# Local attention on one core: scores and values two units at a time, and another order of the softmax steps

## The chip, the cores and the metric

The kernel runs on one core of one Trainium2 chip. The metric is the device time of one execution in microseconds (us), the median of several. Three runs of the kernel before gave 1345.87, 1345.98 and 1346.46 us.

## The reference, cut to what matters

Two layers over 512 tokens of width 1024, float32. Layer 0 mixes tokens with a Mamba-2 scan, layer 1 with the local attention below. Both layers also attend to 256 memory tokens (4 heads of 128), project the joined outputs back and add a squared-ReLU MLP. The change is in layer 1, with one line in layer 0.

```python
# q (b, 8 chunks, 64 queries, 4 kv heads, 4 q heads each, 64); kb, vb: own and previous chunk (128 keys)
scores = jnp.einsum("bcqkgd,bcjkd->bkgcqj", qb, kb) * (64 ** -0.5) + bias   # keys before 0: -inf
m = jnp.maximum(jnp.max(scores, axis=-1, keepdims=True), sink)
p = jnp.exp(scores - m)
denom = jnp.sum(p, axis=-1, keepdims=True) + jnp.exp(sink - m)
out = jnp.einsum("bkgcqj,bcjkd->bcqkgd", p / denom, vb)
# mixed = concat(out, memory attention) @ w_out, w_out 1536 x 1024
```

## The kernel before, in words

Each engine has one hand-ordered stream of instructions, and the streams meet at semaphores.

**Projections.** A float32 matrix product is made of three float32r products: high times high, high times low, low times high. Weights come in panels of 128x1024 elements: a DMA fills `raw` (two buffers), ScalarE rounds it into `whi` (line 557), VectorE subtracts to get `wlo` (line 1098), both three panels ahead of use (`ahead`). TensorE works a panel as four **slots**, one for each PSUM bank G[0] to G[3], six matmuls of 512 columns each (line 1696). After each slot `after_bank` may insert other work; its slot number counts from the first slot of block `B_QB`. Slots 0 to 15 project the second half of the queries, 16 to 31 the memory queries, 32 to 55 the output projection `swa_w_out`, which from slot 32 reads attention outputs as its still operand. A bank can be started anew only when its last result is copied out (`bank_free`): for the queries by lines 1571 (VectorE) and 1023 (ScalarE), for the memory queries by line 1030 (ScalarE).

**Local attention, placed between the slots.** A **unit** u (0 to 15) is one chunk of 64 queries for eight of the 16 heads: `hf, c = divmod(u, 8)`. The first chunk has 64 keys, others 128. Its steps are:

- scores, TensorE (line 2143): four matmuls into the first halves of X[0] and X[1]; float32, two records each, on 64 rows of the array;
- scaling and bias, VectorE (line 1603), from X into `sc[u % 2]`; it waits for the transposes of unit u - 2, which read the same buffer;
- maximum and its negatives, VectorE (lines 1611 to 1614);
- exponentials with sums, ScalarE (lines 998 and 1000);
- division, VectorE (lines 1620 to 1622);
- transposes, TensorE (line 2170), into X[2], and the copy into `pT[u % 2]`, ScalarE (line 1014);
- values, TensorE (line 2159), into the first half of X[3]; float32, on 64 columns of the array;
- the outputs' high part, ScalarE (line 1007), and low part, VectorE (line 1590), which are read by the output projection.

**Order.** `W_TURN` puts turn u behind slot 6 + 2u. In turn u TensorE does the scores of u + 2, the values of u - 1 and the transposes of u. VectorE does scaling and maximum of u + 1 (with the low part of u - 2 between them), then the division of u, then the weight piece `wlo` if the turn is the panel's first. ScalarE does the exponentials of u + 1, the weight piece `whi`, the high part of u - 1 and the copy into `pT` of u. The query copies at slots 14 and 16 (`Q_OUT`) and the memory query copies at slots 30 and 32 (`QM_OUT`) come last in their turns on ScalarE; on VectorE those at 14 and 16 stand behind the division. A panel's first turn is the one at slot 4k, with odd u. The memory attention starts behind slot 38.

**Layer 0.** Behind the slots of its output projection the gated outputs are transposed, a tile f at a time, through the one bank X[3] (`y0_tile`, line 1969). ScalarE takes the high part (line 791), VectorE the low part (`y0_lo`, line 1314), and the next tile waits for that. Steps of the memory attention (`memory_step`) go on between them.

Of the kernel before, what the change touches and what calls it, by code (L numbers as in the profile page):

```python
# [31 lines left out]
P = 128  # L32
# [50 lines left out]
Y0_SLOT = {(44 + f, 0): f for f in range(9)} | {(53, 1): 9, (53, 3): 10, (54, 1): 11}  # L83
MA_STEP = {(53, 1): 0, (54, 0): 1, (54, 3): 2, (55, 2): 3, (56, 1): 4, (57, 0): 5, (57, 2): 6, (58, 0): 7}
# [34 lines left out]
W_FIRST = {1: 0, 2: 1}  # L119
# [19 lines left out]
def build(nc, a, out):  # L139
    ctx = ExitStack()  # L140
    with ctx:
# [213 lines left out]
        def _(sp):  # L355
# [110 lines left out]
            for n in range(12):  # L466
                load(v[n % 6, n // 6], B_W1 + n // 4, n % 4)
                if n == 7:
                    sp.wait_ge(a_o, 2 * NCH)
                    gains("norm_mix_post", "norm_mlp_pre", 1, 1)  # L470
# [72 lines left out]
        def _(act):  # L543
# [460 lines left out]
            def w_out(u):  # L1004
                hf, c = divmod(u, NCH)
                act.wait_ge(a_o, u + 1)
                act.activation(y1hi[:, 4 * hf:4 * hf + 4, CH * c:CH * c + CH],
                               X[3][:, 0:256].rearrange("p (r q) -> p r q", r=4), ACT.Copy).then_inc(a_hi, 1)
# [24 lines left out]
            def attention_panel(blk, q):  # L1033
# [6 lines left out]
                for slot in range(first, first + 4):  # L1040
                    if W_FIRST.get(slot) == 0:
                        w_exp(0)
                    u = W_TURN.get(slot)
                    if u is not None:
                        if u + 1 < 2 * NCH:
                            w_exp(u + 1)
# [3 lines left out]
                        if u >= 1:  # L1050
                            w_out(u - 1)
                        w_turned(u)
                    if slot == W_LAST:
                        w_out(2 * NCH - 1)
# [29 lines left out]
        def _(dve):  # L1084
# [283 lines left out]
            def mixer_out_panel(q):  # L1368
# [8 lines left out]
                for b in range(4):  # L1377
# [4 lines left out]
                    f = Y0_SLOT.get((4 * B_W0 + q, b))  # L1382
# [203 lines left out]
            def w_lo(u):  # L1586
                hf, c = divmod(u, NCH)
                where = (slice(None), slice(4 * hf, 4 * hf + 4), slice(CH * c, CH * c + CH))
                dve.wait_ge(a_hi, u + 1)
                dve.tensor_tensor(y1lo[where], X[3][:, 0:256].rearrange("p (r q) -> p r q", r=4),  # L1590
                                  y1hi[where].bitcast(F32), ALU.subtract).then_inc(a_lo, 1)

            def w_scores(u):
# [3 lines left out]
                cols, heads = slice(4 * u, 4 * u + 4), slice(4 * hf, 4 * hf + 4)  # L1597
                dve.wait_ge(a_s, u + 1)
                if u >= 2:
                    dve.wait_ge(a_tr, u - 1)  # L1600
                for g in range(2):
                    s = X[g][:, 0:256].rearrange("p (r n) -> p r n", r=2)
# [5 lines left out]
                if u >= 3:  # L1608
                    w_lo(u - 3)
# [15 lines left out]
            def attention_panel(blk, q):  # L1625
# [6 lines left out]
                for slot in range(first, first + 4):  # L1632
                    if W_FIRST.get(slot) == 0:
                        w_scores(0)
# [620 lines left out]
```

## Time and profile before

| | |
|---|---|
| median of three runs | 1345.98 us (1345.87 to 1346.46) |
| the profiled execution's own time | 1347.32 us |
| its span, first to last instruction | 1345.6 us |
| TensorE busy (PE) | 1330.5 us, 99% of the span |
| VectorE busy (DVE) | 688.0 us, 51% |
| ScalarE busy (ACT) | 586.6 us, 44% |
| GpSimd busy (POOL) | 124.4 us, 9% |
| mean granted TensorE clock | 0.999 |
| chain that ended last | PE 85%, DVE 8%, ACT 4% of the span |

A group's name is line, engine, operation and tile. A busy TensorE counts every matmul from its start to its modelled end, and neighbours overlap. The distance between two starts is what a matmul costs, not its length: a float32r matmul of 512 columns has a record of 0.39 us. An idle time in brackets is what the engine spent with nothing running, and behind the arrow stands what ended it.

### The profile page before, as it was taken

How to read it: one execution, taken by the hardware profiler on the slowest of the kernel's cores; microseconds unless marked ns; L12 is line 12 of the kernel's file. 1: busy time of each engine (PE TensorE's matmuls, PEld its weight loads, DVE VectorE, ACT ScalarE, POOL GpSimd, SP SyncE). 2: the span in 40 equal slices, each digit the busy share in tenths (PEclk: the TensorE clock that was granted, in tenths of full speed). 3: DMA queues.
4: the chain of work that ended last, by engine and by line, in shares of the span. 5: the costliest groups of instructions: out<-in, count | busy, mean ns of one | idle time of the engine just before them, and what ended most of it. 6: DMA issues, size and time to landing. Idle time of an engine off the chain costs nothing.

```text
span 1345.6 us, 18412 instructions
## 1 busy us (share of the span) xinstructions
PE 1330.5 (99%) x6943; PEld 1095.9 (81%) x6943; DVE 688.0 (51%) x1085; ACT 586.6 (44%) x1107; POOL 124.4 (9%) x131
## 2 busy tenths in 40 slices
PE   9999999999999999999999999999999999999998
PEld 7777778887788888888888897777898888888886
DVE  5586677886437543223443364765374432244333
ACT  6645455686435443213432244665364332234321
POOL 0045352761000000000000000000000000000000
PEclk9999999999999999999999999999999999999999
DMA  6343433343432323242232233112223323332231
GB/s 211 97 132 102 124 98 99 108 161 110 157 110 79 98 90 108 94 126 94 94 110 88 69 117 99 51 60 79 78 65 108 109 95 117 102 94 94 94 99 74
DMA packets 75551, 137.75 MB, mean 102 GB/s; under 512 B 6342, under 2 KB 16854, under 8 KB 75478
## 3 DMA queue, kind: packets, MB, share of 16 engines
q1 hardware_dynamic: 71184, 134.76, 31.0%
q10 hardware_dynamic: 4294, 2.00, 0.8%
q8 instruction: 48, 0.79, 0.2%
q14 instruction: 25, 0.20, 0.0%
HBM read 133.41 MB, written 2.93 MB: 101 GB/s over the span
## 4 chain that ended last, share of the span: by engine, by line
PE 85%; DVE 8%; ACT 4%; issue 2%; POOL 1%; DMA 1%; DVEq 0%; ACTq 0%; POOLq 0%
PE G L1696 54%; PE X L1696 12%; PE X L1719 7%; PE G L1769 3%; PE X L1769 3%; DVE conv L1237 2%; PE X L1883 1%; PE X L1874 1%; ACT whi L557 1%; PE X L1957 1%; DVE wlo L1098 1%; ACT sc L1000 1%; DVE sc L1603 1%; PE X L1896 1%; DVE satt L1611 1%
## 5 line engine op out<-in xcount | busy, mean ns | idle before, releaser
L1098 DVE TENSOR_TENSOR wlo<-raw,whi 128x1024 fp32r<-128x1024 f32 x223 | 274.7, 1237 | 458.6 <-ACT whi L557 457.7
L557 ACT ACTIVATE whi<-raw 128x1024 fp32r<-128x1024 f32 x223 | 234.7, 1059 | 429.0 <-PE G L1696 216.3
L1696 PE MATMUL G<-uhi,whi 128*128 128x512 f32 x736 | 294.4, 400 | 1.1 <-DVE sz L1225 0.6
L1696 PE MATMUL G<-uhi,wlo 128*128 128x512 f32 x736 | 287.1, 390 | 0.0
L1696 PE MATMUL G<-ulo,whi 128*128 128x512 f32 x736 | 286.6, 389 | 0.0
L1696 PEld LDWEIGHTS G<-uhi,whi 128*128 128x128 f32 x736 | 138.3, 188 | 31.9 <-issue 2.1
L1696 PEld LDWEIGHTS G<-uhi,wlo 128*128 128x128 f32 x736 | 138.2, 188 | 29.5
L1696 PEld LDWEIGHTS G<-ulo,whi 128*128 128x128 f32 x736 | 138.4, 188 | 28.3
L1696 PE MATMUL G<-whi,hidhi 128*128 128x512 f32 x256 | 99.6, 389 | 0.0
L1696 PE MATMUL G<-whi,hidlo 128*128 128x512 f32 x256 | 99.6, 389 | 0.0
L1696 PE MATMUL G<-wlo,hidhi 128*128 128x512 f32 x256 | 99.6, 389 | 0.0
L518 POOL TENSOR_SCALAR csrow<-csrow,small 128x128 f32<-128x128 f32 x96 | 92.4, 980 | 4.9 <-DMA csrow<-cs_rows 4.9
L1696 PE MATMUL X<-whi,hidhi 128*128 128x512 f32 x192 | 74.7, 389 | 0.0
L1696 PE MATMUL X<-whi,hidlo 128*128 128x512 f32 x192 | 74.7, 389 | 0.0
L1696 PE MATMUL X<-wlo,hidhi 128*128 128x512 f32 x192 | 74.7, 389 | 0.0
L1517 DVE TENSOR_TENSOR hidlo<-sq,hidhi 128x512 f32 x56 | 37.5, 690 | 56.5 <-ACT hidhi L952 56.5
L948 ACT ACTIVATE sq<-og 128x512 f32<-128x512 f32 x56 | 34.9, 632 | 68.1 <-DVE og L1513 68.1
L1696 PEld LDWEIGHTS G<-whi,hidhi 128*128 128x128 f32 x256 | 48.1, 188 | 10.0
L1696 PEld LDWEIGHTS G<-wlo,hidhi 128*128 128x128 f32 x256 | 48.1, 188 | 10.0
L1696 PEld LDWEIGHTS G<-whi,hidlo 128*128 128x128 f32 x256 | 48.1, 188 | 9.9
L1696 PEld LDWEIGHTS X<-whi,hidhi 128*128 128x128 f32 x192 | 36.0, 188 | 7.5
L1696 PEld LDWEIGHTS X<-wlo,hidhi 128*128 128x128 f32 x192 | 36.0, 188 | 7.5
(339 smaller groups left out, 2217.7 us busy)
## 6 DMA issues: line engine op xcount, KB each, us to landing
raw<-in_w_up SPq DMA_DIRECT2D x64, 512.0 KB, 3.8
raw<-in_w_down SPq DMA_DIRECT2D x64, 512.0 KB, 3.5
raw<-in_ssd_w_in SPq DMA_DIRECT2D x20, 512.0 KB, 3.6
raw<-in_w_mem_kv SPq DMA_DIRECT2D x16, 512.0 KB, 3.5
raw<-in_ssd_w_out SPq DMA_DIRECT2D x16, 512.0 KB, 3.5
raw<-in_swa_w_in SPq DMA_DIRECT2D x16, 512.0 KB, 3.8
raw<-in_ssd_w_in SPq DMA_DIRECT2D x16, 384.0 KB, 3.4
csrow<-cs_rows SPq DMA_DIRECT2D x16, 384.0 KB, 4.4
```

The source lines that it names most:

```text
L518: seg = ps.tensor_scalar(csrow[v % 3][:, h, :], csrow[v % 3][:, h, :], small[:, R_SUM, x:x + 1], 0.0, ALU.subtract, ALU.min)
L557: act.activation(whi[q][:, :, :], raw[q % 2][:, :, :], ACT.Copy).then_inc(hi_done, 1)
L948: act.activation(sq[b % 2][:, :], og[b % 2][:, :], ACT.Square).then_inc(hidsq_done, 1)
L1000: act.activation(sc[u % 2][:, r, 0:w], sc[u % 2][:, r, 0:w], ACT.Exp, bias=satt[:, 1, 4 * u + r:4 * u + r + 1], accum_out=satt[:, 3, 4 * u ...
L1098: dve.tensor_tensor(wlo[q][:, :, :], raw[q % 2][:, :, :], whi[q][:, :, :].bitcast(F32), ALU.subtract).then_inc(lo_done, 1)
L1237: dve.scalar_tensor_tensor(out=c, in0=xconv[o][:, b, 0:T - (TAPS - 1 - w)], scalar=conv_w[:, w, ch:ch + 1], in1=c, op0=ALU.mult, op1=ALU.a ...
L1517: dve.tensor_tensor(hidlo[:, j, b, :], sq[b % 2][:, :], hidhi[:, j, b, :].bitcast(F32), ALU.subtract).then_inc(hid_done, 1)
L1603: biased = dve.scalar_tensor_tensor(out=sc[u % 2][:, 2 * g:2 * g + 2, 0:w], in0=s[:, :, 0:w], scalar=float(CH) ** -0.5, in1=bias[:, 4 * hf ...
L1611: link(dve.tensor_reduce(satt[:, 0, cols], sc[u % 2][:, :, 0:w], AX.X, ALU.max))
L1696: mm = pe.matmul(o, st, mv, start=(kt == 0 and fresh and not go_on), stop=(q == total - 1 and k == 1), skip_group_check=True)
L1719: mm = pe.matmul(o, st, mv, start=False, stop=(x == 3 and k == 1), skip_group_check=True)
L1769: mm = pe.matmul(o, st, mv, start=(q == 0 and k == 0 and fresh), stop=(q == 3 and k == 1), skip_group_check=True)
```

## The change

Scores of two units (2j and 2j + 1, `S_AT`) are issued together, behind slot 1 and then behind slots 4j + 3, between the turns. They use both halves of X[0] and X[1], and VectorE is told only when both are done. Values of two units are issued together in the even turns from 2 on, in front of the transposes, into all of X[3]; each matmul writes two runs of 64 columns, 128 apart. Their outputs' high and low parts are taken by one instruction each of 512 columns. On VectorE the order in a turn becomes: scaling of u + 1, low part (in odd turns), division of u, maximum of u + 1, query copies, weight piece. On ScalarE it becomes: weight piece, high part (in even turns), copy into `pT` of u, exponentials of u + 1, query and memory query copies. In layer 0 the low part of tile 10 moves behind the memory step at panel 54, slot 0, on VectorE alone.

```diff
--- before.py
+++ after.py
@@ -81,6 +81,8 @@
 CONV_IN = {1: 0, 2: 1, 4: 2, 6: 3, 8: 4}
 MEM_AT = {29 + 11 * i + r: (i, r) for i in range(2) for r in range(4)}
 Y0_SLOT = {(44 + f, 0): f for f in range(9)} | {(53, 1): 9, (53, 3): 10, (54, 1): 11}
+Y0_LO = Y0_SLOT | {(54, 0): 10}
+del Y0_LO[53, 3]
 MA_STEP = {(53, 1): 0, (54, 0): 1, (54, 3): 2, (55, 2): 3, (56, 1): 4, (57, 0): 5, (57, 2): 6, (58, 0): 7}
 
 
@@ -116,7 +118,7 @@
 
 
 SLOT0 = 4 * B_QB
-W_FIRST = {1: 0, 2: 1}
+S_AT = {1: 0} | {4 * j + 3: j for j in range(1, NCH)}
 W_TURN = {6 + 2 * u: u for u in range(2 * NCH)}
 W_LAST = 38
 Q_OUT = {14: 0, 16: 1}
@@ -466,7 +468,7 @@
             for n in range(12):
                 load(v[n % 6, n // 6], B_W1 + n // 4, n % 4)
                 if n == 7:
-                    sp.wait_ge(a_o, 2 * NCH)
+                    sp.wait_ge(a_o, NCH)
                     gains("norm_mix_post", "norm_mlp_pre", 1, 1)
             mlp(1, B_F1)
 
@@ -1001,11 +1003,11 @@
                                    bias=satt[:, 1, 4 * u + r:4 * u + r + 1],
                                    accum_out=satt[:, 3, 4 * u + r:4 * u + r + 1]).then_inc(a_exp, 1)
 
-            def w_out(u):
-                hf, c = divmod(u, NCH)
-                act.wait_ge(a_o, u + 1)
-                act.activation(y1hi[:, 4 * hf:4 * hf + 4, CH * c:CH * c + CH],
-                               X[3][:, 0:256].rearrange("p (r q) -> p r q", r=4), ACT.Copy).then_inc(a_hi, 1)
+            def w_out(j):
+                hf, t = divmod(j, NCH // 2)
+                act.wait_ge(a_o, j + 1)
+                act.activation(y1hi[:, 4 * hf:4 * hf + 4, P * t:P * t + P],
+                               X[3][:, :].rearrange("p (r q) -> p r q", r=4), ACT.Copy).then_inc(a_hi, 1)
 
             def w_turned(u):
                 w = P if u % NCH else CH
@@ -1038,20 +1040,20 @@
                     ahead(*todo)
                     todo = None
                 for slot in range(first, first + 4):
-                    if W_FIRST.get(slot) == 0:
+                    if S_AT.get(slot) == 0:
                         w_exp(0)
                     u = W_TURN.get(slot)
                     if u is not None:
-                        if u + 1 < 2 * NCH:
-                            w_exp(u + 1)
                         if todo is not None:
                             ahead(*todo)
                             todo = None
-                        if u >= 1:
-                            w_out(u - 1)
+                        if u % 2 == 0 and u >= 2:
+                            w_out(u // 2 - 1)
                         w_turned(u)
+                        if u + 1 < 2 * NCH:
+                            w_exp(u + 1)
                     if slot == W_LAST:
-                        w_out(2 * NCH - 1)
+                        w_out(NCH - 1)
                     if slot in Q_OUT:
                         queries(N_QB, B_QB, 1, 2 * Q_OUT[slot] + 1)
                     if slot in QM_OUT:
@@ -1379,7 +1381,7 @@
                     if n is not None:
                         memory_step(0, mp0, ymhi0, ymlo0, BM, n, todo)
                         todo = None
-                    f = Y0_SLOT.get((4 * B_W0 + q, b))
+                    f = Y0_LO.get((4 * B_W0 + q, b))
                     if f is not None and f >= 9:
                         y0_lo(f)
                 if todo is not None:
@@ -1583,30 +1585,33 @@
             link(dve.tensor_scalar(sinkb[:, 1, :], sinkb[:, 0, :], -1.0, None, ALU.mult))
             dve.wait_ge(bias_in, 32)
 
-            def w_lo(u):
-                hf, c = divmod(u, NCH)
-                where = (slice(None), slice(4 * hf, 4 * hf + 4), slice(CH * c, CH * c + CH))
-                dve.wait_ge(a_hi, u + 1)
-                dve.tensor_tensor(y1lo[where], X[3][:, 0:256].rearrange("p (r q) -> p r q", r=4),
+            def w_lo(j):
+                hf, t = divmod(j, NCH // 2)
+                where = (slice(None), slice(4 * hf, 4 * hf + 4), slice(P * t, P * t + P))
+                dve.wait_ge(a_hi, j + 1)
+                dve.tensor_tensor(y1lo[where], X[3][:, :].rearrange("p (r q) -> p r q", r=4),
                                   y1hi[where].bitcast(F32), ALU.subtract).then_inc(a_lo, 1)
 
-            def w_scores(u):
+            def w_biased(u):
 
                 hf, c = divmod(u, NCH)
                 w = P if c > 0 else CH
-                cols, heads = slice(4 * u, 4 * u + 4), slice(4 * hf, 4 * hf + 4)
-                dve.wait_ge(a_s, u + 1)
+                dve.wait_ge(a_s, u // 2 + 1)
                 if u >= 2:
                     dve.wait_ge(a_tr, u - 1)
                 for g in range(2):
-                    s = X[g][:, 0:256].rearrange("p (r n) -> p r n", r=2)
+                    s = X[g][:, 256 * (u % 2):256 * (u % 2) + 256].rearrange("p (r n) -> p r n", r=2)
                     biased = dve.scalar_tensor_tensor(out=sc[u % 2][:, 2 * g:2 * g + 2, 0:w], in0=s[:, :, 0:w],
                                                       scalar=float(CH) ** -0.5,
                                                       in1=bias[:, 4 * hf + 2 * g:4 * hf + 2 * g + 2, P - w:P],
                                                       op0=ALU.mult, op1=ALU.add)
                 biased.then_inc(a_sb, 1)
-                if u >= 3:
-                    w_lo(u - 3)
+
+            def w_maxima(u):
+
+                hf, c = divmod(u, NCH)
+                w = P if c > 0 else CH
+                cols, heads = slice(4 * u, 4 * u + 4), slice(4 * hf, 4 * hf + 4)
                 dve.wait_ge(a_sb, u + 1)
                 link(dve.tensor_reduce(satt[:, 0, cols], sc[u % 2][:, :, 0:w], AX.X, ALU.max))
                 link(dve.scalar_tensor_tensor(out=satt[:, 1, cols], in0=satt[:, 0, cols], scalar=-1.0,
@@ -1630,23 +1635,25 @@
                     ahead(*todo)
                     todo = None
                 for slot in range(first, first + 4):
-                    if W_FIRST.get(slot) == 0:
-                        w_scores(0)
+                    if S_AT.get(slot) == 0:
+                        w_biased(0)
+                        w_maxima(0)
                     u = W_TURN.get(slot)
                     if u is not None:
                         if u + 1 < 2 * NCH:
-                            w_scores(u + 1)
-                        else:
-                            w_lo(u - 2)
+                            w_biased(u + 1)
+                        if u % 2 == 1 and u >= 3:
+                            w_lo((u - 3) // 2)
                         w_norm(u)
+                        if u + 1 < 2 * NCH:
+                            w_maxima(u + 1)
                         if slot in Q_OUT:
                             queries(N_QB, B_QB, 1, 2 * Q_OUT[slot])
                         if todo is not None:
                             ahead(*todo)
                             todo = None
                     if slot == W_LAST:
-                        w_lo(2 * NCH - 2)
-                        w_lo(2 * NCH - 1)
+                        w_lo(NCH - 1)
                     if slot == M_FIRST[0]:
                         maxima(1, X, 0)
                     n = M_TURN.get(slot)
@@ -2128,37 +2135,40 @@
             split(1, N_KV, B_KV, half_keys_values, F_KV)
             gemm(N_QA, B_QA, 4, weights_still(u_of), u_wait(U0[3]), bank(F_QA))
 
-            def w_scores(u):
-                hf, c = divmod(u, NCH)
-                if u % NCH == 0:
+            def w_scores(j):
+                hf, c0 = divmod(2 * j, NCH)
+                if c0 == 0:
                     for x in range(4):
                         pe.wait_ge(bank_free[x], F_QA + hf + 1)
-                if u >= 1:
-                    pe.wait_ge(a_sb, u)
-                w = P if c > 0 else CH
-                for r in range(2):
+                if j >= 1:
+                    pe.wait_ge(a_sb, 2 * j)
+                for c in (c0, c0 + 1):
+                    w = P if c > 0 else CH
+                    for r in range(2):
+                        for g in range(2):
+                            kv = slice(CH * g, CH * g + CH)
+                            col = 256 * (c % 2) + P * r
+                            st = qT[kv, 2 * hf + r, c, :, :].rearrange("p s q -> p (s q)")
+                            mm = pe.matmul(X[g][:, col:col + w], st, kT[kv, hf, CH * c + CH - w:CH * c + CH],
+                                           start=True, stop=True)
+                mm.then_inc(a_s, 1)
+
+            def w_values(j):
+                hf, c0 = divmod(2 * j, NCH)
+                pe.wait_ge(a_pT, 2 * j + 2)
+                if j >= 1:
+                    pe.wait_ge(a_lo, j)
+                if j == 1:
+                    pe.wait_ge(v2_done, 32)
+                for c in (c0, c0 + 1):
+                    w = P if c > 0 else CH
+                    vals = V if c % 2 or c == 0 else V2
                     for g in range(2):
-                        kv = slice(CH * g, CH * g + CH)
-                        st = qT[kv, 2 * hf + r, c, :, :].rearrange("p s q -> p (s q)")
-                        mm = pe.matmul(X[g][:, P * r:P * r + w], st, kT[kv, hf, CH * c + CH - w:CH * c + CH],
-                                       start=True, stop=True)
-                mm.then_inc(a_s, 1)
-
-            def w_values(u):
-                hf, c = divmod(u, NCH)
-                w = P if c > 0 else CH
-                pe.wait_ge(a_pT, u + 1)
-                if u >= 1:
-                    pe.wait_ge(a_lo, u)
-                if u == 2:
-                    pe.wait_ge(v2_done, 32)
-                vals = V if c % 2 or c == 0 else V2
-                for g in range(2):
-                    kv = 2 * hf + g
-                    for s in range(2):
-                        mm = pe.matmul(X[3][CH * s:CH * s + CH, P * g:P * g + P],
-                                       vals[0:w, c // 2, CH * kv:CH * kv + CH],
-                                       pT[u % 2][0:w, 2 * g:2 * g + 2, s, :], start=True, stop=True)
+                        kv = 2 * hf + g
+                        for s in range(2):
+                            o = X[3][CH * s:CH * s + CH, :].rearrange("p (r c q) -> p r c q", r=4, c=2)
+                            mm = pe.matmul(o[:, 2 * g:2 * g + 2, c % 2, :], vals[0:w, c // 2, CH * kv:CH * kv + CH],
+                                           pT[c % 2][0:w, 2 * g:2 * g + 2, s, :], start=True, stop=True)
                 mm.then_inc(a_o, 1)
 
             def w_transposes(u):
@@ -2175,21 +2185,19 @@
 
                 def after_bank(q, b):
                     slot = 4 * (4 * blk + q - SLOT0) + b
-                    u = W_FIRST.get(slot)
-                    if u is not None:
-                        if u == 0:
+                    j = S_AT.get(slot)
+                    if j is not None:
+                        if j == 0:
                             pe.wait_ge(half_k, 2)
                             pe.wait_ge(half_v, 2)
-                        w_scores(u)
+                        w_scores(j)
                     u = W_TURN.get(slot)
                     if u is not None:
-                        if u + 2 < 2 * NCH:
-                            w_scores(u + 2)
-                        if u >= 1:
-                            w_values(u - 1)
+                        if u % 2 == 0 and u >= 2:
+                            w_values(u // 2 - 1)
                         w_transposes(u)
                     if slot == W_LAST:
-                        w_values(2 * NCH - 1)
+                        w_values(NCH - 1)
                     if slot == M_FIRST[0]:
                         for x in range(4):
                             pe.wait_ge(bank_free[x], F_Q1 + 1)
@@ -2202,7 +2210,7 @@
                         if n == 0:
                             pe.wait_ge(a_pT, 2 * NCH)
                         if n == 2:
-                            pe.wait_ge(a_lo, 2 * NCH)
+                            pe.wait_ge(a_lo, NCH)
                         memory_step(1, mp1, mpT1, qmT1, X, n)
                     if slot == M_LAST:
                         memory_values(1, mpT1, X, MH - 1)
@@ -2218,7 +2226,7 @@
 
             def y1_wait(kt):
                 if kt < 8:
-                    pe.wait_ge(a_lo, NCH * (1 + kt // 4))
+                    pe.wait_ge(a_lo, NCH // 2 * (1 + kt // 4))
                 else:
                     pe.wait_ge(ma_lo, 4 + kt - 8 + 1)
```

## Rows read from the trace of the kernel before

**Rows 1.** The page's costliest groups: busy us, mean ns of one, idle before.

```profile
L1098 DVE TENSOR_TENSOR wlo<-raw,whi 128x1024 fp32r<-128x1024 f32 x223 | 274.7, 1237 | 458.6 <-ACT whi L557 457.7
```

**Rows 2.** Waits from 836 to 914 us, then TensorE's timeline: start us, us.

```profile
PE X L2170 <- DVE sc L1622: 3.9, 6, 0.8
...
827.72 0.66 PE L2143 MATMUL X<-kT,qT 64*128 64x64 f32 x8
...
913.46 1.13 PE L1874 MATMUL X<-memKT,qmT 128*128 128x256 f32 x4
```

**Rows 3.** TensorE's timeline in turn 1: start us, us, operands.

```profile
839.65 0.39 PE L1696 MATMUL G<-ulo,whi 128*128 128x512 f32 x1
839.88 0.39 PE L1696 MATMUL G<-uhi,wlo 128*128 128x512 f32 x1
840.20 0.72 PE L2143 MATMUL X<-kT,qT 64*128 64x128 f32 x8
840.84 0.65 PE L2159 MATMUL X<-pT,V 64*64 64x128 f32 x8
841.42 0.66 PE L2170 MATMUL X<-ident,sc 128*128 128x128 f32 x4
...
842.15 0.39 PE L1696 MATMUL G<-ulo,whi 128*128 128x512 f32 x1
```

**Rows 4.** The same view, narrower: the last four and two score records.

```profile
840.52 0.39 PE L2143 MATMUL X<-kT,qT 64*128 64x128 f32 x4
...
840.63 0.28 PE L2143 MATMUL X<-kT,qT 64*128 64x128 f32 x2
```

**Rows 5.** TensorE's timeline, a score group between plain slots.

```profile
829.90 0.72 PE L2143 MATMUL X<-kT,qT 64*128 64x128 f32 x8
...
830.88 0.39 PE L1696 MATMUL G<-ulo,whi 128*128 128x512 f32 x1
```

**Rows 6.** TensorE's timeline, the transposes of turn 10.

```profile
885.88 0.66 PE L2170 MATMUL X<-ident,sc 128*128 128x128 f32 x4 [0.65 <-DVE sc L1622]
```

**Rows 7.** VectorE's timeline in turn 10.

```profile
882.76 0.75 DVE L1603 SCALAR_TENSOR_TENSOR sc<-X,bias 128x256 f32<-128x256 f32 x2
...
883.75 0.68 DVE L1611 TENSOR_REDUCE satt<-sc 128x4 f32<-128x512 f32 x1
...
884.74 0.15 DVE L1620 TENSOR_TENSOR satt<-satt 128x4 f32<-128x4 f32 x1
...
885.14 0.69 DVE L1622 TENSOR_TENSOR sc<-sc,satt 128x512 f32<-128x512 f32 x1
```

**Rows 8.** ScalarE's timeline in turn 12.

```profile
894.72 0.21 ACT L998 ACTIVATE satt<-satt 128x4 f32<-128x4 f32 x1 [2.52 <-DVE satt L1614]
...
896.38 0.36 ACT L1007 ACTIVATE y1hi<-X 128x256 fp32r<-128x256 f32 x1
896.64 0.57 ACT L1014 ACTIVATE pT<-X 128x512 f32<-128x512 f32 x1
897.12 1.06 ACT L1030 ACTIVATE qmT<-G 128x512 f32<-128x512 f32 x2
```

**Rows 9.** One line's instructions (min/median/max ns); VectorE's timeline at slot 16.

```profile
L1204 DVE TENSOR_TENSOR ymlo<-X,ymhi x8: 683/692/692, 346.7 to 948.5; 128x512 fp32r<-128x512 f32 x8
...
860.77 1.39 DVE L1571 COPY qT<-G 64x512 f32<-64x512 f32 x2
```

**Rows 10.** Layer 0: TensorE's timeline, then ScalarE's.

```profile
334.80 0.66 PE L1896 MATMUL X<-ident,mp 128*128 128x128 f32 x4 [0.90 <-DVE mp L1213]
...
336.68 0.60 PE L1969 MATMUL X<-ident,sz 128*128 128x128 f32 x4
...
331.68 0.69 ACT L791 ACTIVATE y0hi<-X,par 128x512 fp32r<-128x512 f32 x1 [2.36 <-PE X L1969]
333.99 0.47 ACT L631 ACTIVATE mp<-X,msum 128x256 f32<-128x256 f32 x1 [1.62 <-DVE msum L1200]
...
334.90 1.05 ACT L557 ACTIVATE whi<-raw 128x1024 fp32r<-128x1024 f32 x1
```

## The prediction, made before the changed kernel ran

> **What bounds the kernel now.** I read the page's busy times first: TensorE is busy for 99% of the span at the full clock. So only two things can move the time: what the streams on TensorE cost, and the few places where it waits. The list of waits comes second. From 836 to 914 us, the local attention, TensorE's transposes wait six times for VectorE's division, 3.9 us in all and 0.8 at most [rows 2]. Layer 0 has one wait of 0.90 us for a division of the memory attention [rows 10]. Third come the timelines of the three engines over two turns, for the chain behind such a wait. VectorE's division of unit 10 ends at 885.14 + 0.69 = 885.83, and the transposes start at 885.88 [rows 6, 7]. The turn's VectorE row starts with scaling and maximum of unit 11, and the division of unit 10, on which TensorE depends, stands behind them.
>
> **TensorE's own work.** Prices are distances between starts. A plain matmul is 0.23 us (839.65 to 839.88), a slot of six 1.38. Entering attention work costs 0.32 - 0.23 = 0.09. A score group is 0.64, a value group 0.58, and transposes with the way back 842.15 - 841.42 - 0.23 = 0.50 [rows 3]. A turn with all three is 0.09 + 0.64 + 0.58 + 0.50 = 1.81. A score group alone is 830.88 - 829.90 - 0.23 + 0.09 = 0.84 [rows 5]. Two more score matmuls (a pair of records) cost 0.11 [rows 4]. So four pairs are 0.44 of the 0.64, and the rest is the change of the array's tile form. I give the value pairs the same 0.11.
>
> - Before: 2 score groups alone (1.68), turn 0 (1.23), turns 1 to 13 at 1.81 (23.53), turns 14 and 15 without scores at 1.17 (2.34), last values 0.67: 29.45 us.
> - After: 8 double score groups at 0.84 + 0.44 = 1.28 (10.24), 9 turns of transposes alone at 0.59 (5.31), 7 with double values at 0.09 + 0.58 + 0.44 + 0.50 = 1.61 (11.27), last values 1.11: 27.93 us.
>
> **The merging saves 1.5 us of TensorE.** It isn't more, since the scores lose their place next to the values and pay an entry and an exit of their own.
>
> **The waits before, as a sum.** First scores to first memory scores is 913.46 - 827.72 = 85.74 us [rows 2]. Of this 37 slots take 51.06 and the work above, less its first entry, 29.36. The rest, 5.3 us, is waiting, and it includes the 3.9. This is what the new order can give back at most.
>
> **The waits after.** I follow the new order through one pair of turns.
>
> - Division of u now waits only for its exponentials and the scaling of u + 1, not for the maximum. In even turns the scaled scores are there, and the division is done 4.1 us after the last transposes (worked out below), while TensorE comes back after 4.4. So it is not kept waiting there: 5.3 us go.
> - In odd turns something else is late. The scaling of u + 1 needs the double scores that TensorE issues only one slot before the turn, and VectorE is in order: scaling, low part of 512 columns, division. From the start of the double scores: the last record starts 0.43 + 0.44 = 0.87 later and is 0.28 long [rows 3, 4], so VectorE starts at about 1.20. Scaling takes 0.66 to the next start (its record is 0.75). The low part takes 0.6 (0.69 for this form, less some overlap). The division is 885.83 - 884.74 = 1.09 and the way to TensorE 0.05 [rows 7, 9]. Sum 3.6 us. TensorE is back for the transposes after 0.64 + 0.44 + 0.11 + 1.38 + 0.09 = 2.66. **It waits 0.94 us.** This holds for turns 3, 5, 9 and 11 (3.8 us). Turn 1 has no low part (0.34), turn 7 scales a narrow unit (0.69), turn 13 is relieved by a wait just ahead of it (0.54). Together 5.3 us.
> - Turn 15 has no scores. Its division waits for exponentials that now stand behind the copy into pT: transposes of 14 to ScalarE 0.70, copy 0.48, exponentials 896.38 - 894.72 = 1.66 plus 0.1 until the sum is read, division 1.09, handovers 0.1: 4.1 us to the next transposes [rows 6 to 8]. TensorE needs 0.50 + 2.76 + 0.09 = 3.35. Wait 0.8.
> - The query copies move behind the maximum. At slot 16 VectorE's pair, 1.39 us [rows 9], starts 0.9 after the transposes' start (maximum: 884.74 - 883.75 = 0.99 behind a division that ended 0.05 earlier [rows 7]) and ends 2.3 after it. TensorE reaches slot 18, which needs that bank, after 0.50 + 1.38 = 1.88: wait 0.44. VectorE's delay also holds up the division of turn 6, 0.41 more.
> - The memory query copies move behind the exponentials on ScalarE. From a turn's transposes: 0.70 + 0.48 + 1.66 + one copy of about 0.55 (half of 1.06) + 0.05 = 3.44 [rows 8]. Behind slot 32 the bank is needed by slot 34, at 1.87: **wait 1.58**. Behind slot 30 the double scores lie between, and the bank of slot 32 is late by only 0.4.
>
> The new waits are 5.3 + 0.8 + 0.44 + 0.41 + 0.4 + 1.58 = 8.9 us. In the attention this makes 8.9 - 5.3 - 1.5 = **2.1 us more**.
>
> **Parts without a cost.** ScalarE's weight piece (1.05 [rows 10]) stands in front of the pT copy in odd turns. It runs while the division (1.09) and the transposes (0.70) run, and would cost up to 1 us a turn without that cover. The weight pieces are two panels ahead of use, so their new places and VectorE's 1.24 [rows 1] hold nothing up. The DMA queue (SP) waits for those pieces, and for the last values before it loads the gains, which are issued behind the same slot 38 as before. One instruction of 512 columns for two of 256 saves VectorE and ScalarE some time, which lies beside TensorE's. POOL has no part.
>
> **Layer 0.** The low part of tile 10 no longer stands in front of the memory step, so the 0.90 us wait goes. It now comes behind that step: the high part starts at 331.68 and takes 0.69, exponentials 334.90 - 333.99 = 0.91, whi 1.05, wlo 1.24 less an overlap of 0.1, low part 0.7. That ends at 336.2. Tile 11's transposes wait for it and started at 336.68 before [rows 1, 10]. **Gain 0.4 us**, between 0 (if it isn't overlapped) and 0.9.
>
> **The sum.** 1347.32 (the profiled execution's own) + 2.1 - 0.4 = 1349.0. That execution is 1.34 above the median, so on the median's scale the time is **1347.7 us**, 0.13% more. The bounds of what no row shows: a double group's further pairs could cost 0.05 less or 0.1 more each (±1 us over all), the low part of 512 columns 0.33 to 0.75, handovers ±0.05 for each of some ten waits, layer 0 as said. Together about -1.3 and +1.5.
>
> **The rivals.**
>
> 1. *The copies don't hold a bank.* If slots 18, 32 and 34 find their banks free, 2.8 us go: 1344.9. For it: in the trace of before they hold nearly nothing. Against: exponentials of 1.66 us now stand ahead of them. Chance 8%.
> 2. *TensorE's waits vanish*, since the double scores' results reach VectorE in time: -5.3 - 1.5 - 0.4 gives 1338.8. For it: VectorE and ScalarE are busy for half of the time. Against: one slot is 1.38 us, and scores to division is 3.6. Chance 7%.
> 3. *The values' output in two runs is slow*, the rival on the other side. If each pair of value records took 0.22 in place of 0.11, a double group would cost 0.88 more. Its place is in front of the transposes, where TensorE's stream alone sets the pace until the next scores, so eight times 0.88 lands on the path: 1347.7 + 7.0 = 1354.7. It decides from 0.016 us a pair, which over 64 pairs is the 1.0 us up to what can be measured. For it: no row here has such an output. Against: these matmuls already read their moving operand in two runs of 64, and a group of eight records is 0.58 [rows 3]. Chance 7%. The Trainium skill (PSUM — Partial Sum Buffer, "Specifications (TRN2)") speaks for this rival: "any non-contiguous AP slows matmuls significantly". It gives no factor, and no run here shows it yet.
>
> **How the numbers follow.** The forecast has 78%, and 1346.4 to 1349.2 as its own range. About 0.2%, or 2.7 us, can be told from no change: that is 1343.3 to 1348.7. Of the forecast's 78%, 14 lie above 1348.7, as its bounds say. With rival 3 this gives slower 21%, with rival 2 faster 7%, and 72% are left for the same. The range, 1344.6 to 1350.0, holds the forecast and rival 1, and leaves out rivals 2 and 3 and the tails.
>
> **What would show it.** The double score group: 1.1 us between its first start and the next slot. Transposes of turns 3, 5, 9 and 11 with 0.8 to 1 us of idle before them, ended by VectorE's division, and none in even turns but turn 6. The output projection's slot 34 late by 1.5 us for ScalarE's line 1030. First to memory scores 87.8 us in place of 85.74. In layer 0 the transposes of tile 11, not those of the memory step, waiting about 0.6. The prediction is wrong if odd turns don't wait, or if the values' pairs are farther apart than 0.11 us.

## The result, and the profile after

| | before | after |
|---|---|---|
| median of 17 runs each | 1346.5 us (1345.84 to 1348.04) | 1348.74 us (1348.09 to 1350.1; a single one of 3384) |
| ratio, with its 95% interval | | 1.0016 (1.0009 to 1.0024) |
| profiled span | 1345.6 us | 1347.9 us |
| TensorE busy | 1330.5 us | 1329.4 us |
| first scores to first memory scores | 85.75 us | 88.46 us |
| memory scores to memory scores around panel 54, layer 0 | 6.99 us | 6.64 us |

The changed kernel is 2.2 us slower, 0.16%. Two stretches hold the whole change: +2.71 and -0.35 make +2.36, against 2.3 in the spans. The rest is the same to 0.04 us: from that step of layer 0 to the first local scores it is 487.84 us in both, and from the first memory scores of layer 1 to TensorE's end 426.70 and 426.67.

The timeline of TensorE in the changed kernel, for the two ends of the attention stretch. They answer to the last two of [rows 2]; the merged score group now shows sixteen records, of the narrow unit 0 and of unit 1.

```profile
827.35 1.16 PE L2152 MATMUL X<-kT,qT 64*128 64x64 f32 x16
...
915.82 1.13 PE L1881 MATMUL X<-memKT,qmT 128*128 128x256 f32 x4
```

The list of TensorE's waits (total us, times, longest), which answers to the first of [rows 2]. The transposes waited 3.9 us there, in even turns. Now they wait 5.9 us, in all odd turns and in turn 6, and two kinds of bank release have joined them. One kind has gone: in the kernel before, the scores of unit 8 waited once for the query copies (line 1023), 0.5 us.

```profile
PE X L2180 <- DVE sc L1627: 5.9, 9, 0.9
PE G L1703 <- ACT qmT L1032: 1.8, 2, 1.4
...
PE X L1976 <- DVE y0lo L1316: 0.6, 1, 0.6
...
PE G L1703 <- DVE qT L1573: 0.4, 1, 0.4
```

Turn 3, TensorE's timeline. The double score group starts at 846.83, and the slot behind it 1.09 later. The transposes wait 0.88 for VectorE.

```profile
846.83 1.16 PE L2152 MATMUL X<-kT,qT 64*128 64x128 f32 x16
847.92 0.50 PE L1703 MATMUL G<-uhi,whi 128*128 128x512 f32 x1
...
850.45 0.66 PE L2180 MATMUL X<-ident,sc 128*128 128x128 f32 x4 [0.88 <-DVE sc L1627]
```

VectorE's timeline beside it. Scaling starts 1.21 us after the scores' first matmul, the low part follows, and the division, 849.31 to 850.40, comes behind it. This is what [rows 7] showed in another order.

```profile
848.04 0.76 DVE L1604 SCALAR_TENSOR_TENSOR sc<-X,bias 128x256 f32<-128x256 f32 x2 [2.64 <-PE X L2152]
848.71 0.68 DVE L1592 TENSOR_TENSOR y1lo<-X,y1hi 128x512 fp32r<-128x512 f32 x1
849.31 0.15 DVE L1625 TENSOR_TENSOR satt<-satt 128x4 f32<-128x4 f32 x1
...
849.71 0.69 DVE L1627 TENSOR_TENSOR sc<-sc,satt 128x512 f32<-128x512 f32 x1
```

Slot 34: TensorE's timeline, then ScalarE's. The transposes of turn 13 start at 901.25. ScalarE does the exponentials from 902.44 and only then the copies (line 1032). The slot starts at 904.71, 3.46 us after the transposes. Its second matmul comes 0.34 later, where neighbours inside a slot are 0.23 apart. It answers to [rows 8], where the copies came directly behind the pT copy.

```profile
901.25 0.66 PE L2180 MATMUL X<-ident,sc 128*128 128x128 f32 x4 [0.45 <-DVE sc L1627]
...
904.71 0.50 PE L1703 MATMUL G<-whi,y1hi 128*128 128x512 f32 x1 [1.41 <-ACT qmT L1032]
905.05 0.40 PE L1703 MATMUL G<-whi,y1lo 128*128 128x512 f32 x1
...
902.44 0.20 ACT L1000 ACTIVATE satt<-satt 128x4 f32<-128x4 f32 x1
...
904.07 1.06 ACT L1032 ACTIVATE qmT<-G 128x512 f32<-128x512 f32 x2
```

Layer 0, TensorE's timeline, against [rows 10]. The memory step's transposes wait no more, and tile 11's wait 0.57.

```profile
333.73 0.60 PE L1903 MATMUL X<-ident,mp 128*128 128x128 f32 x4
...
336.29 0.63 PE L1976 MATMUL X<-ident,sz 128*128 128x128 f32 x4 [0.57 <-DVE y0lo L1316]
```

### The profile page after: what moved, and what is told of

It is laid out like the page before. It is cut to its first block, busy times and chain, and to the rows that moved or that the text cites. A ratio compares the mean times of both kernels' runs of the same rounds, so it can differ in the third digit from the quotient of the medians.

```text
span 1347.9 us, 18388 instructions
## 1 busy us (share of the span) xinstructions
PE 1329.4 (99%) x6943; PEld 1094.8 (81%) x6943; DVE 687.3 (51%) x1077; ACT 586.3 (43%) x1099; POOL 122.8 (9%) x131
## 3 DMA queue, kind: packets, MB, share of 16 engines
HBM read 133.41 MB, written 2.93 MB: 101 GB/s over the span
## 4 chain that ended last, share of the span: by engine, by line
PE 89%; DVE 7%; ACT 2%; issue 1%; DMA 0%; DVEq 0%; ACTq 0%
PE G L1703 56%; PE X L1703 12%; PE X L1726 7%; PE G L1776 3%; PE X L1776 3%; DVE conv L1239 2%; PE X L1890 1%; PE X L1881 1%; PE X L1964 1%; DVE wlo L1100 1%; PE X L2152 1%; PE X L2180 1%; PE X L2170 1%; ACT conv L671 1%; PE X L1903 0%
## 5 line engine op out<-in xcount | busy, mean ns | idle before, releaser
L1703 PEld LDWEIGHTS X<-whi,hidlo 128*128 128x128 f32 x192 | 36.0, 188 | 7.5
```

What stands on the lines that cost most here:

```text
L1703: mm = pe.matmul(o, st, mv, start=(kt == 0 and fresh and not go_on), stop=(q == total - 1 and k == 1), skip_group_check=True)
```

## The experiments

Each ran five rounds beside the kernel before. "Stretch" is the time from first scores to first memory scores in the trace; the changed kernel and experiment 9, which do the same there, agree to 0.02 us (88.46 and 88.48). The medians of whole runs are coarser: kernels with the same stretch differ by up to 0.7 us in them. Three questions were put: is it the merging or the order that costs, where does each wait come from, and does the two-run output of the values cost anything.

| kernel | stretch | median, us | ratio to before, 95% |
|---|---|---|---|
| before | 85.75 | 1346.1 to 1346.5 | |
| changed | 88.46 | 1348.74 | 1.0016 (1.0009 to 1.0024) |
| 1 merging alone | 101.30 | 1361.23 | 1.0112 (1.0096 to 1.0127) |
| 2 order alone | 85.20 | 1345.54 | 0.9995 (0.9986 to 1.0004) |
| 3 scores one slot earlier | 81.95 | 1342.61 | 0.9973 (0.9961 to 0.9984) |
| 4 memory query copies split | 86.98 | 1347.10 | 1.0008 (0.9999 to 1.0017) |
| 5 values' output contiguous | 88.45 | 1349.47 | 1.0022 (1.0013 to 1.0031) |
| 6 = 3 and 4 | 80.10 | 1340.26 | 0.9955 (0.9941 to 0.9969) |
| 7 = 2 and 4 | 82.55 | 1343.00 | 0.9978 (0.9969 to 0.9987) |
| 8 unit 8's values over 128 rows | 88.32 | 1348.65 | 1.0016 (1.0007 to 1.0025) |
| 9 layer 0 put back | 88.48 | 1349.37 | 1.0023 (1.0014 to 1.0032) |
| 10 query copies first | 88.48 | 1349.00 | 1.0022 (1.0012 to 1.0032) |

### 1. Merging alone

```diff
 VectorE, in a turn, after the scaling and the low part
-w_norm(u)
-if u + 1 < 2 * NCH: w_maxima(u + 1)
+if u + 1 < 2 * NCH: w_maxima(u + 1)
+w_norm(u)
 ScalarE: w_exp(u + 1) in front of the weight piece instead of behind w_turned(u)
```

> The changed kernel with its double score and value groups, but VectorE's and ScalarE's order as before (maximum of u + 1 in front of the division of u; exponentials of u + 1 first on ScalarE). My theory: merging alone is a loss, since the double scores come only one slot ahead of the odd turn and then scaling, low part, maximum and division stand in a row; every turn waits 1.5 to 1.9 us. First scores to first memory scores about 101 us (before: 85.7, changed: 88.5), the time 13 us above the changed kernel, about 1362. Rival, that the new order is what costs and merging is harmless: the stretch at or under 86 us, the time at or under 1346.

The stretch is 101.30 us, as expected. Double groups in the old order are a clear loss, so the new order is not what costs: it takes back 12.8 of the 15.5 us that the double groups lose. The list of waits, and a table of stretches of time (span, busy us of TensorE, its weight loads, VectorE, ScalarE and GpSimd, then the granted clock):

```profile
PE X L2180 <- DVE sc L1627: 15.8, 11, 1.9
...
855.00:859.00 4.00, 2.67 (x26) 1.99 (x25) 3.81 (x11) 1.86 (x10) 0.00 (x0) 1.00 0.40 131
859.00:863.00 4.00, 3.90 (x28) 2.68 (x26) 2.06 (x5) 1.92 (x4) 0.00 (x0) 1.00 0.00 0
863.00:867.00 4.00, 2.23 (x8) 1.94 (x9) 3.50 (x9) 3.24 (x11) 0.00 (x0) 0.75 0.00 0
867.00:871.00 4.00, 4.00 (x28) 2.99 (x27) 3.40 (x9) 2.61 (x11) 0.00 (x0) 0.83 0.39 133
871.00:880.00 9.00, 7.66 (x48) 5.76 (x46) 4.40 (x12) 4.42 (x15) 0.00 (x0) 1.00 0.01 2
...
888.00:892.00 4.00, 3.34 (x11) 2.77 (x12) 2.25 (x4) 2.80 (x10) 0.00 (x0) 0.61 0.00 0
...
896.00:905.00 9.00, 7.13 (x39) 5.40 (x38) 5.12 (x13) 3.27 (x12) 0.00 (x0) 0.86 0.01 2
```

The long waits brought something unforeseen. TensorE's granted clock fell to a mean of 0.75 and 0.83 in the pieces from 863 to 871 (part of each at 1.2 GHz, the rest at 2.4), and it was back at 1.00 behind them. In the two pieces before, TensorE was busy for 2.67 and 3.90 us, and it had just waited 1.9 us when the lower clock set in. It fell again from 888 us and from 902 us on, each time behind another wait of 1.87; two more waits of 1.86, at 852.41 and 913.89, had no such fall behind them. By the starts in the timeline, the slots took 4.34 us in place of 2.93 for twelve matmuls, but the double value group behind them took 1.02 in place of 2.42, since the wait in it was gone. So the slower clock mostly filled time in which TensorE would have waited. It cost little: VectorE's divisions of units 6, 10 and 12 ended at 870.60, 894.36 and 907.07, and their transposes started at 870.74, 894.77 and 907.31. Beyond the usual 0.05 these are 0.1, 0.4 and 0.2 us.

### 2. The order alone

```diff
 (kernel before, single groups) VectorE, in a turn
-w_scores(u + 1)  # scaling, low part of u - 2, maximum
-w_norm(u)
+w_scores(u + 1)  # scaling only
+if u >= 2: w_lo(u - 2)
+w_norm(u)
+if u + 1 < 2 * NCH: w_maxima(u + 1)
 ScalarE: weight piece, high part, w_turned(u), and only then w_exp(u + 1)
```

> The kernel before with single groups, but in the new order: low part and division of u in front of the maximum of u + 1, exponentials of u + 1 last in ScalarE's turn. My theory: all waits of the transposes but one small one go, and in their place come two of 1.6 us for the memory query copies (slots 32 and 34) and 0.8 for the query copies. The stretch 84.6 us, the time 1.1 us below before, 1345.4. Rival, that the odd turns' waits of the changed kernel come from the order and not from the scores' place: transposes of turns 3, 5, 9 and 11 wait about 0.9 here too, and the stretch is at least 88 us.

```profile
PE G L1702 <- ACT qmT L1030: 2.9, 2, 1.5
PE X L2149 <- ACT qT L1023: 0.9, 1, 0.9
```

Not one wait of the transposes is left in the list, in odd or even turns. So the odd turns' waits of the changed kernel don't come from the order; experiment 3 shows that they come from where its scores stand. In place of the transposes' waits TensorE waits 2.9 us for the memory query copies, and the scores (line 2149) wait once for the query copies, 0.9 in place of 0.5. That uses up nearly all that the order gave back: the stretch is 85.20, where 84.6 was expected, and the interval of the ratio includes 1.

### 3. Scores one slot earlier

```diff
-S_AT = {1: 0} | {4 * j + 3: j for j in range(1, NCH)}
+S_AT = {1: 0} | {4 * j + 2: j for j in range(1, NCH)}
 TensorE, in turn u (even)
 w_transposes(u)
+if j: w_scores(j)
```

> The changed kernel with the double scores one slot earlier, directly behind the transposes of the even turn (slots 4j + 2 in place of 4j + 3), nothing else. My theory: the 0.96 us waits of turns 3, 5, 9 and 11, and those of 1, 7 and 13, go, and an entry and an exit less per pair of turns saves TensorE some 0.1 each. The query copies' waits stay and a part moves to the next turns. The stretch 82.0 us, 6.5 less than in the changed kernel, the time 1342.3. Rival, that the odd turns wait for exponentials or weight pieces and not for scores: the stretch within 1 us of 88.5.

The list of waits, and turns 4 and 5 in TensorE's timeline:

```profile
PE G L1703 <- ACT qmT L1032: 1.6, 2, 1.4
PE X L2180 <- DVE sc L1627: 1.1, 2, 0.7
PE G L1703 <- DVE qT L1573: 0.3, 1, 0.3
...
852.50 0.66 PE L2180 MATMUL X<-ident,sc 128*128 128x128 f32 x4
853.09 1.16 PE L2152 MATMUL X<-kT,qT 64*128 64x128 f32 x16
...
856.81 0.39 PE L1703 MATMUL G<-uhi,wlo 128*128 128x512 f32 x1
857.04 0.60 PE L2180 MATMUL X<-ident,sc 128*128 128x128 f32 x4
857.40 0.48 PE L1703 MATMUL G<-uhi,whi 128*128 128x512 f32 x1
857.71 0.40 PE L1703 MATMUL G<-ulo,whi 128*128 128x512 f32 x1
```

The odd turns' transposes start without a wait (857.04). The two waits that are left are those of turn 6 and of turn 15, which has no scores. 88.46 falls to 81.95, as expected. The one slot, 1.38 us, was more than the 0.96 that was missing.

### 4. The memory query copies split

```diff
 ScalarE, in a turn
 w_turned(u)
+if slot in QM_OUT: memory_queries(2 * QM_OUT[slot])
 if u + 1 < 2 * NCH: w_exp(u + 1)
 if slot in QM_OUT:
-    for b in range(2): memory_queries(2 * QM_OUT[slot] + b)
+    memory_queries(2 * QM_OUT[slot] + 1)
```

> The changed kernel with one of the two memory query copies at slots 30 and 32 in front of the exponentials on ScalarE, the other behind them. My theory: the waits at slots 32 (0.5 us) and 34 (1.7 us) go, and 0.5 us comes back since the exponentials are later: the stretch 87.2 us in place of 88.5, the time 1347.4. Rival, that those banks are held by the attention and not by the copies: no change.

```profile
PE X L2181 <- DVE sc L1628: 6.3, 9, 0.9
PE G L1704 <- DVE qT L1574: 0.4, 1, 0.4
```

The 1.8 us for line 1032 is gone from the list, and the transposes' waits rise from 5.9 to 6.3. The stretch falls by 1.48.

### 5. The values' output contiguous

```diff
-o = X[3][64 * s:64 * s + 64, :].rearrange("p (r c q) -> p r c q", r=4, c=2)  # writes o[:, 2g:2g+2, c % 2, :]
+o = X[3][64 * s:64 * s + 64, 256 * (c % 2) + 128 * g:256 * (c % 2) + 128 * g + 128]
 evictions: X[3] read as "p (c r q) -> p r c q", y1hi and y1lo written as "p r (c q) -> p r c q"
```

> The changed kernel with each value matmul writing one run of 128 columns (unit even in the first half of X[3], odd in the second), and the two evictions reading and writing with one more dimension instead. My theory: the two runs cost TensorE nothing; a double value group stays at 1.02 us (1.17 with a narrow unit), the stretch from first scores to first memory scores at 88.5, the time at 1348.7. By my third rival and the Trainium skill (PSUM — Partial Sum Buffer, Specifications (TRN2)), which says that a non-contiguous pattern slows matmuls, the group gets shorter than 1.02 and the stretch by eight times as much.

The double value group in the changed kernel, from its first matmul to the transposes', and the same here:

```profile
853.78 1.09 PE L2170 MATMUL X<-pT,V 128*64 128x128 f32 x16
...
854.81 0.66 PE L2180 MATMUL X<-ident,sc 128*128 128x128 f32 x4
```

```profile
852.54 1.09 PE L2172 MATMUL X<-pT,V 128*64 128x128 f32 x16
...
853.57 0.66 PE L2182 MATMUL X<-ident,sc 128*128 128x128 f32 x4
```

Both take 1.03 us, and the stretches agree to 0.01. Two runs of 64 columns cost what one of 128 does. The sentence of the Trainium skill (PSUM — Partial Sum Buffer, "Specifications (TRN2)") that any non-contiguous pattern slows matmuls significantly does not hold for this one; other patterns were not tried. The evictions with the extra dimension took no longer either (0.60 us for the high part and 0.68 for the low part in both).

### 6. Both edits: scores earlier, memory query copies split

```diff
 (the edits of experiments 3 and 4)
-S_AT = {1: 0} | {4 * j + 3: j for j in range(1, NCH)}
+S_AT = {1: 0} | {4 * j + 2: j for j in range(1, NCH)}
+if slot in QM_OUT: memory_queries(2 * QM_OUT[slot])  # in front of w_exp
```

> The changed kernel with both edits: double scores directly behind the even turn's transposes, and one of two memory query copies in front of the exponentials. My theory: the edits take away different waits and nearly add up. From 81.95 us with the scores moved alone, the stretch falls by 1.5 to 80.4, the time to 1341.1. Left are about 0.6 and 0.4 for the query copies at slot 16 and turn 6, 0.2 and 0.3 in turns 13 and 14, 0.8 in turn 15. Rival, that with the scores moved the copies' wait turns into waits of turns 14 and 15: stretch 81.5 or more.

```profile
PE X L2181 <- DVE sc L1628: 1.1, 2, 0.7
PE G L1704 <- DVE qT L1574: 0.3, 1, 0.3
```

The stretch is 80.10 us, and the time 1340.26: 0.45% below before, and its interval lies wholly below 1. It beats both kernels. From 3 the copies' split brings 1.85 us and not 1.5. The rival, that their wait would turn into waits of turns 14 and 15, falls.

### 7. Single groups, new order, copies split

```diff
 (the kernel before, with the edits of experiments 2 and 4)
+if slot in QM_OUT: memory_queries(2 * QM_OUT[slot])  # in front of w_exp
```

> Single groups in the new order (as in the run with the order alone) and the memory query copies split around the exponentials. My theory: the two 1.6 us waits at slots 32 and 34 go and 0.7 comes back: the stretch falls from 85.2 to 82.9, the time to 1343.2. Against the combined kernel this prices the double groups themselves: 2.5 us of stretch, made of TensorE's form changes, if they are placed well. Rival, that double groups are worth nothing once the waits are gone: both stretches within 0.7 us.

```profile
PE X L2150 <- ACT qT L1023: 0.9, 1, 0.9
PE X L2177 <- DVE sc L1626: 0.5, 1, 0.5
```

82.55 us. Against 6 the double groups are worth 2.45 us of stretch. The lists of waits hold 1.4 us in both kernels, so this is in the main TensorE's own work, and it is more than the 1.5 that the prediction gave to merging.

The reason lies in one price. The prediction took 0.59 us for transposes that stand alone: 0.50 from rows where they follow values, and 0.09 for an entry. Experiment 3 shows such transposes where nothing waits: they start 0.23 behind a plain matmul (856.81 to 857.04), like another plain one, and cost 857.71 - 857.04 - 0.23 = 0.44. Scores directly behind the transposes save nothing more: 853.09 - 852.50 = 0.59 there, and apart it is the transposes' 0.41, a way back of 0.09 and an entry of 0.09, the same 0.59.

### 8. Unit 8's values over 128 rows

```diff
-w = P if c > 0 else CH
+w = P if c > 0 or hf else CH
```

> The changed kernel, where the value matmuls of unit 8 run over 128 rows in place of 64 (they add stale rows, so unit 8's output is not the reference's). In the changed kernel the double value groups that hold a narrow unit take 1.17 us, the others 1.02. Theory: a change of the array's rows inside the group costs 0.15; here the group of units 8 and 9 falls to 1.02, that of 0 and 1 stays at 1.17, the stretch falls by 0.15. Rival, that it is the first group of each half for another reason (new weights, bank): both stay at 1.17.

TensorE's timeline, the values of units 8 and 9 up to the transposes, first in the changed kernel, then here:

```profile
884.51 1.24 PE L2170 MATMUL X<-pT,V 64*64 64x128 f32 x16
...
885.68 0.66 PE L2180 MATMUL X<-ident,sc 128*128 128x128 f32 x4
```

```profile
883.59 1.09 PE L2170 MATMUL X<-pT,V 128*64 128x128 f32 x16
...
884.61 0.66 PE L2180 MATMUL X<-ident,sc 128*128 128x128 f32 x4
```

1.17 us fall to 1.02, and the group of units 0 and 1 keeps its 1.17. A change from 64 to 128 rows inside a group costs 0.15. The narrow form by itself doesn't: in the kernel before, a value group on 64 rows took 0.58 us (turn 1) and one on 128 rows 0.59 (turn 3).

### 9. Layer 0 put back

```diff
-f = Y0_LO.get((4 * B_W0 + q, b))
+f = Y0_SLOT.get((4 * B_W0 + q, b))
```

> The changed kernel with the low part of tile 10 in layer 0 back in its old place. Theory: the wait of 0.90 us in front of the memory step's transposes comes back and the 0.6 us wait of tile 11's transposes goes; from the memory scores of that step to those of the next it is 6.99 us as before, in place of 6.64: 0.35 us in the trace, too little for the clock on the wall (1349.1). Rival, that the 0.35 us came from somewhere else: no change there.

```profile
333.49 0.66 PE L1903 MATMUL X<-ident,mp 128*128 128x128 f32 x4 [0.90 <-DVE mp L1215]
...
335.37 0.60 PE L1976 MATMUL X<-ident,sz 128*128 128x128 f32 x4
```

The 0.90 us wait is back, and from memory scores to memory scores it is 7.00 us. The move is worth 0.35 us in the trace. The medians, 1349.37 against 1348.74, can't resolve it.

### 10. The query copies first

```diff
 VectorE, in a turn
 w_norm(u)
+if slot in Q_OUT: queries(N_QB, B_QB, 1, 2 * Q_OUT[slot])
 if u + 1 < 2 * NCH: w_maxima(u + 1)
-if slot in Q_OUT: queries(N_QB, B_QB, 1, 2 * Q_OUT[slot])
```

> The changed kernel with VectorE's query copies at slots 14 and 16 in front of the maximum again. Theory: the wait of 0.67 us at slot 18 goes, but the maximum of unit 6 and so its exponentials and division are 1.4 us later, so the 0.44 us wait of turn 6 grows to 1.0 or more: the stretch stays within 0.3 us of 88.5. Rival, that the copies' new place cost 1.1 us outright: the stretch falls to 87.4.

```profile
862.54 1.09 PE L2170 MATMUL X<-pT,V 128*64 128x128 f32 x16
...
864.65 0.66 PE L2180 MATMUL X<-ident,sc 128*128 128x128 f32 x4 [1.02 <-DVE sc L1627]
```

Slot 18 waits no more, and the values and their wait in turn 6 grow from 1.46 to 2.11 us. The stretch stays at 88.48. The 1.1 us there is what 1.39 us of copies cost in VectorE's chain, in both of the places tried.

## Why the prediction was right

The forecast was 1.7 us more, on the median's scale. Measured were 2.2, and 2.36 in the trace. The forecast of 1347.7 us stood on a median of 1345.98; with all runs the kernel before has 1346.5, which is half of what separates 1347.7 from 1348.74. The waits, their places and their causes were foreseen. One price was wrong, and that it did no harm was luck: nothing in the prediction had looked for it. Point by point:

- **Where the waits are.** Every wait that was named is there, and no other in the attention. Turns 1 to 13, the odd ones, waited 0.36, 0.96, 0.96, 0.69, 0.96, 0.96 and 0.49 us beyond the 2.66 that the prediction gave to TensorE's own work, 5.4 against 5.3 in all. Turn 15 waited 0.77 against 0.8, turn 6 0.44 against 0.41. Experiment 3 shows that the scores' place makes the odd ones, and 2 that the order doesn't.
- **The banks.** From the transposes to the start of slot 34 3.46 us were measured, and 3.44 forecast until its bank is free; to slot 18 it was 2.41 against 2.3. The toll was larger all the same: 0.48, 1.72 and 0.67 in place of 0.4, 1.58 and 0.44. This was **mis-sized**, by 0.45 us together. About half of it is that I took the wait for the whole price: slots 18 and 34 also start slower, 905.05 - 904.71 = 0.34 in place of 0.23. The rest is that slot 18 started 0.1 later than reckoned, and 0.08 at slot 32, where the scores stand between and the slower start is paid anyway.
- **What merging saves.** 27.93 us of work were forecast, 1.5 less than before. The double groups cost what was said: 1.09 us from the scores' start to the next slot, and 1.02 for the values. But the term of nine turns of transposes alone was **mis-sized**: 0.59 each, where experiment 3 has 0.44, so 1.35 too much. Two narrow value groups cost 0.15 each more (experiment 8). So TensorE's own work fell by an estimated 1.5 + 1.35 - 0.3 = 2.55 us, and experiments 6 and 7 measured 2.45. **The forecast was saved by its own sum:** in eight of the nine turns VectorE's division decides when the transposes start, and what TensorE saves ahead of it becomes waiting. Counted against TensorE's true work, each of those waits is 0.1 to 0.15 longer than above. That the stretch less 37 slots and the waits above, 88.46 - 51.06 - 9.46 = 27.94, agrees with the forecast's 27.84 is no check of the prices, since those waits were counted with the same prices.
- **Layer 0.** 0.35 against 0.4 us; tile 11 waits in the place of the memory step, as said (experiment 9).
- **The rivals.** The copies do hold their banks (4). TensorE's waits did not vanish. The values' two runs cost nothing, and their pairs are 0.11 apart (5).
- **The place among the bounds.** In the attention 2.71 us against 2.1, the difference being mainly the 0.45 of the banks above. Slower is now told from no change, though less than the 0.2% that I had set as what can be told.

## What to carry to other kernels

Two groups merged save only entries and ways back, here about 2.5 us over sixteen units, and they delay the first half of their results until the second is there. Work out for each merged group who waits for its signal and how far away the place is where the result is needed; moving the same group one slot ahead turned a loss of 2.7 us into a gain of 3.8. And where a step is moved behind a long one on an engine, follow every small copy that ends up behind it: the memory query copies, 1.1 us in each of two turns, cost 2.2 us because they free a bank, and splitting them gave 1.5 to 1.85 of it back. And price a step from rows where it has the neighbours that it will have: transposes that were priced at 0.59 us from rows behind values cost 0.44 alone.

## What the runs showed of the hardware

- TensorE pays for a start after a wait on a bank beyond the wait: 0.34 us to the second matmul in place of 0.23 (904.71 to 905.05). It isn't the wait alone: behind a double score group, where nothing waits, it is 0.34 too (847.92 to 848.26).
- Four transposes that stand alone between slots of 512-column matmuls cost 0.44 us where nothing waits (experiment 3, 857.04 to 857.71), and 0.50 where they follow values (in the kernel before, turn 1).
- A change of the number of rows, 64 to 128, between matmuls of one group costs 0.15 us (experiment 8). At a change of form the last record of one form is 0.20 before the first of the next, and the second pair 0.15 to 0.21 behind the first, where later pairs within a group are 0.11 apart.
- A matmul that writes two runs of 64 columns, 128 apart, into a bank is as fast as one that writes 128 in a row: 1.03 us for a double group both ways (experiment 5).
- In experiment 1 TensorE's granted clock fell from 1.00 to 0.75 and 0.83 over 8 us, part of them at 1.2 GHz, and matmuls were 0.43 us apart there in place of 0.23. It fell twice more in that stretch. No single wait ahead of any of the falls was longer than 1.9 us, and two waits as long had no fall behind them. In the changed kernel, with waits of 0.9 at most in the odd turns and of 1.4 once, it was 1.00 from 836 to 914 us.
